# Hybrid attention trunk on one core: psT from three banks to two, psO from one bank to two

## The chip, the cores and the metric

The kernel runs on one core of one Trainium2 chip. The metric is device time in microseconds (us), lower is better; the time before is the median of 3 runs. A profile is one execution of its own, with the time of each instruction on each engine. PE is TensorE, DVE is VectorE, ACT is ScalarE, POOL is GpSimd, SP is SyncE, which here issues nearly all the DMAs.

## The reference

One layer over x of 1024 tokens by 1024 features, fp32. Three groups of 8 heads of size 64 share one input projection and one output projection:

```python
h = rmsnorm(x, norm_g)
proj = h @ w_in                 # q, k, v, gate for each group, forget logits for one
o_sb = stick_breaking_attention(q_sb, k_sb, v_sb)           # strictly causal
o_ch = chunked_relpos_attention(norm(q_ch), norm(k_ch), v_ch, rel_bias)   # a band of 9 chunks of 64
o_fx = forgetting_attention(norm(q_fx), norm(k_fx), v_fx, log_f)          # causal, with decay
mixed = concat(o_g * silu(gate_g) for g in (sb, ch, fx))
out = x + mixed @ w_out
```

In each attention a weight matrix of queries by keys (scores, then a softmax or the stick-breaking product) multiplies the values of its head.

## The kernel before

**High and low halves.** To keep fp32 accuracy, each matrix is held as a rounded high part and a low part (the fp32 value less the high part). ACT copies the high part out, DVE subtracts it from the source and writes the low part. So each tile that PE has turned (transposed) into PSUM is read twice, first by ACT and then by DVE, and is free only when DVE has ended.

**Pairs, rows and units.** The 24 heads are 12 pairs `j` of two heads `s`. A pair has 16 score blocks `n` (8 blocks of 128 queries for each head). Four blocks make a unit `u`, of which there are 48; unit `u` belongs to pair `u // 4`. For each unit the weight blocks, 128x128 with queries on the partitions, are turned by PE so that keys lie on the partitions, and then multiplied with the values. `banks(u)` says how: a unit is 3, 5 or 7 tiles of up to four blocks. The steps of a unit stand in this order:

```python
    seq = [("turn", u, 0)]
    for b in range(1, len(banks(u))):
        seq += [("turn", u, b), ("values", u, b - 1)]
    return seq + [("values", u, len(banks(u)) - 1)]
```

**The work of one tile.** `turn` (L1287) is up to four transposes on PE from `z` into `psT`; ACT copies the high part into `pt` (L939), DVE subtracts and writes the low part (L1128) and counts `s_evac`. `values` (L1305) waits for that count and multiplies both parts into the sum bank `psO`. When all tiles of a unit are added, `gather` reads `psO`: ACT takes one half of the partitions to `otmp` (L949), DVE adds the other half (L1135, which counts `s_os`) and multiplies with the gate (L1141).

**Who else uses psT.** All turned tiles take the banks of `psT` in one running order `m`, tile `m` in bank `m % NT`, and before tile `m` PE waits for the DVE reading of tile `m - NT`. There are 290 tiles: 16 of `x` (`("x", t)`, two for each t, transposes L1185, read by ACT L786 and DVE L991), 48 of `heads` (queries and keys, L1235, read by ACT L879 with a gain and by DVE L1053), 2 of `forget` (L1244, ACT L896, DVE L1070) and 224 of `turn`. The `heads` tiles then go through two DMAs inside `stack` (L635, L636, then L642, L643) before scores can use them (L1265, L1266).

**PSUM.** There are eight banks of 128x512 fp32: two for scores (`psS`), three for `psT`, one for `psO`, two for projections and the output (`psP`). At the end the output projection rotates over `psP`, `psS` and `psO` (L1353).

**The order.** `plan()` writes out one order of steps at build time, and each engine goes through the same list, doing its own part of each step, in order. Nothing overtakes. Attention steps have hand-set places (`AT`, `OWN`, `NEXT`), and between them `filler` puts pieces of the next pair's projection (L1213 for q, k, v, L1217 for the gate), three matmuls at a time. At the start, steps stand so: `x` 0 and `x` 1 (four tiles), then the first projection pieces; later `x` 7, `heads` (0,0,0) and `forget` 0 stand one behind the other. In the pairs 1 to 4 the second half of the first head's queries and keys stands inside a unit:

```
turn(3,0)=34, project, turn(3,1)=35, project, heads(1,0,1)=36, values(3,0), scores(18), turn(3,2)=37
```

and the same with the numbers of units 7, 11 and 15. From pair 5 on it stands behind the first `values` of the unit (`values(31,0), heads(8,0,1)=190, scores, turn(31,2)=191, values(31,1), project, turn(31,3)=192`). The number is the place `m` in the order of psT.

Of the kernel before, what the change touches and what calls it, by code (L numbers as in the profile page):

```python
# [6 lines left out]
F32 = mybir.dt.float32  # L7
# [3 lines left out]
ACT = mybir.ActivationFunctionType  # L11
AX = mybir.AxisListType

P = 128
# [15 lines left out]
HALF = 512  # L30
# [14 lines left out]
TOKW = FW + QKV  # L45
WP = TOKW + P
WR = 3
NT = 3
PTR = 2


# [327 lines left out]
def build(nc, x, norm_g, w_in, b_forget, q_norm_ch, k_norm_ch, q_norm_fox, k_norm_fox, rel_bias, w_out, out):  # L379
# [5 lines left out]
    with ExitStack() as ctx:  # L385
# [34 lines left out]
        vst = sb("vst", [P, 3, TT, P], F32R)  # L420
# [6 lines left out]
        otmp = sb("otmp", [P, HALF])  # L427
# [15 lines left out]

        psS = ctx.enter_context(nc.psum_tensor("psS", [P, 2 * HALF], F32))
        psT = ctx.enter_context(nc.psum_tensor("psT", [P, NT, HALF], F32))
        psO = ctx.enter_context(nc.psum_tensor("psO", [P, HALF], F32))
        psP = ctx.enter_context(nc.psum_tensor("psP", [P, 2, HALF], F32))


# [16 lines left out]
        def end_tile(t, c):  # L466
            return piece[3 * c + t] if t < 3 else resid[t][:, c * HALF:(c + 1) * HALF]

        endbank = [psP[:, i, :] for i in range(2)] + [psS[:, i * HALF:(i + 1) * HALF] for i in range(2)] + [psO[:, :]]

        s_const = sem("s_const")
        s_identr = sem("s_identr")
# [43 lines left out]
        s_oc = sem("s_oc")  # L516
        s_os = sem("s_os")
# [240 lines left out]
        def _(act):  # L758
# [6 lines left out]
            for step in PLAN:  # L765
# [27 lines left out]
                if kind == "weights":  # L793
                    _, j, k = step
# [3 lines left out]
                    if j:  # L798
# [3 lines left out]
                                         scale=gcol[:, k:k + 1]).then_inc(s_whi, 1)  # L802
                if kind == "gatew":
                    _, j, h = step
# [21 lines left out]
                if kind == "raw":  # L826
                    _, j, t = step
                    u = t // 4
# [18 lines left out]
                if kind == "gate":  # L847
                    _, j, u = step
# [12 lines left out]
                if kind == "sq":  # L861
                    _, j, u = step
# [6 lines left out]
                if kind == "heads":  # L869
                    _, j, s, u = step  # L870
# [5 lines left out]
                    else:  # L876
# [3 lines left out]
                                         scale=gain[:, g:g + 1]).then_inc(s_hi, 1)  # L880
                if kind == "vsplit":
                    _, j, s, u = step
# [5 lines left out]
                if kind == "forget":  # L888
                    _, u = step
# [11 lines left out]
                if kind == "scores" and step[1] >= NSOFT:  # L901
# [3 lines left out]
                    i = n - NSOFT  # L905
# [19 lines left out]
                if kind == "rescale":  # L925
# [4 lines left out]
                                         scale=small[:, n % 8, 3:4]).then_inc(s_pn, 1)  # L930
                if kind == "turn":
                    _, u, b = step
# [7 lines left out]
                if kind == "gather":  # L940
                    _, u = step
                    s = u // 2 % 2
                    rows, other = slice(s * HD, (s + 1) * HD), slice((1 - s) * HD, (2 - s) * HD)
                    act.wait_ge(s_pv, VAL0[u + 1])
                    if u == 0:
                        act.wait_ge(s_fc, 4)
                    if u >= 1:
                        act.wait_ge(s_prod, u)
                    nc.scalar.activation(otmp[rows, :], psO[other, :], ACT.Copy, scale=0.5).then_inc(s_oc, 1)  # L949
                if kind == "mix":  # L950
                    _, j, u = step
                    i = 2 * j + u
# [9 lines left out]
        def _(dve):  # L962
            for step in PLAN:
# [29 lines left out]
                if kind == "weights":  # L993
                    _, j, k = step
# [3 lines left out]
                                                   scalar=gcol[:, k:k + 1], in1=wpair[0][:, k, FW:TOKW].bitcast(F32),  # L998
# [5 lines left out]
                if kind == "gatew":  # L1004
                    _, j, h = step
# [17 lines left out]
                if kind == "gate":  # L1023
                    _, j, u = step
# [3 lines left out]
                                                   in1=psP[:, u, :], op0=ALU.add, op1=ALU.mult).then_inc(s_gate, 1)  # L1028
                if kind == "sq":
                    _, j, u = step  # L1030
                    i = 2 * j + u
# [6 lines left out]
                if kind == "norm" and step[1] < NORMED:  # L1038
                    _, j, u = step
                    i = 2 * j + u  # L1040
                    dve.wait_ge(s_rn, i + 1)
                    r = rs[:, 16 * u:16 * u + 16].rearrange("p (t f s a) -> p t f s a", t=4, f=2, a=1)
                    for f in range(2):
                        ins = nc.vector.tensor_tensor(qk_out(f, u), qk_raw(f, u),
                                                      r[:, :, f, :, :].broadcast_to([P, 4, 2, HD]), ALU.mult)
                    ins.then_inc(s_qn, 1)
                if kind == "heads":
                    _, j, s, u = step
# [5 lines left out]
                        out=stack[:, s, 2, cols], in0=psT[:, m % NT, :], scalar=gain[:, g:g + 1],  # L1054
                        in1=stack[:, s, 1, cols].bitcast(F32), op0=ALU.mult, op1=ALU.subtract).then_inc(s_evac, 1)
                if kind == "vsplit":
                    _, j, s, u = step
                    h = 2 * j + s
                    i = VSPLIT[j, s, u]
# [3 lines left out]
                if kind == "forget":  # L1063
                    _, u = step
# [7 lines left out]
                if kind == "decay":  # L1072
                    _, u = step
# [9 lines left out]
                if kind == "scores" and step[1] < NSOFT:  # L1083
# [3 lines left out]
                    s = n // TT % 2  # L1087
# [10 lines left out]
                    if n >= 8:  # L1098
# [3 lines left out]
                                                   scalar=3.0e38, op0=ALU.add, op1=ALU.min,  # L1102
# [8 lines left out]
                if kind == "weigh" and step[1] >= NSOFT:  # L1111
                    n = step[1]
                    i = n - NSOFT
# [8 lines left out]
                if kind == "turn":  # L1122
                    _, u, b = step
# [6 lines left out]
                if kind == "gather":  # L1130
                    _, u = step
                    s = u // 2 % 2
                    rows = slice(s * HD, (s + 1) * HD)
                    dve.wait_ge(s_oc, u + 1)
                    nc.vector.scalar_tensor_tensor(out=otmp[rows, :], in0=psO[rows, :], scalar=0.5, in1=otmp[rows, :],  # L1135
                                                   op0=ALU.mult, op1=ALU.add).then_inc(s_os, 1)
                    j, h = u // 4, u % 2
                    cols = slice(h * HALF, (h + 1) * HALF)
                    dve.wait_ge(s_gate, 2 * j + h + 1)
                    dve.wait_ge(s_os, u + 1)  # L1140
                    nc.vector.tensor_tensor(gate[rows, j % 2, cols], gate[rows, j % 2, cols], otmp[rows, :],  # L1141
                                            ALU.mult).then_inc(s_prod, 1)
                if kind == "mix":
                    _, j, u = step
# [3 lines left out]
                if kind == "part":  # L1148
                    i = step[1]
# [23 lines left out]
        def _(pe):  # L1173
            pe.wait_ge(s_identr, 1)
            for step in PLAN:
                kind = step[0]
                if kind == "x":
                    _, t = step
                    pe.wait_ge(s_xn, t + 1)
                    for u in range(2):  # L1180
# [3 lines left out]
                        for i in range(4):  # L1184
                            ins = nc.tensor.transpose(psT[:, m % NT, i * P:(i + 1) * P],  # L1185
                                                      xt[t][:, (4 * u + i) * P:(4 * u + i + 1) * P], ident)
                        ins.then_inc(s_turn, 1)
                if kind == "project":
                    _, j, gi, k0, k1 = step
                    what, i = GROUPS[gi]  # L1190
# [3 lines left out]
                    if k0 == 0 and before >= 0:  # L1194
                        jb, gb = divmod(before, NG)
                        kb, ib = GROUPS[gb]
# [8 lines left out]
                    for k in range(k0, k1):  # L1205
# [4 lines left out]
                        for q, (a, b) in enumerate(((0, 0), (0, 1), (1, 0))):  # L1210
                            if what == "t":
                                first = 0 if j == 0 else FW
                                ins = nc.tensor.matmul(dst[:, 0:TOKW - first], hT[a][:, k, i * P:(i + 1) * P],  # L1213
                                                       wpair[b][:, k, first:TOKW],
                                                       start=(k == 0 and q == 0), stop=(k == KT - 1 and q == 2))
                            else:
                                ins = nc.tensor.matmul(dst[:, :], wpair[b][:, k, TOKW:WP],  # L1217
                                                       hT[a][:, k, i * HALF:(i + 1) * HALF],
                                                       start=(k == 0 and q == 0), stop=(k == KT - 1 and q == 2))
# [6 lines left out]
                if kind == "heads":  # L1226
                    _, j, s, u = step
# [6 lines left out]
                    for i in range(4):  # L1234
                        ins = nc.tensor.transpose(psT[:, m % NT, i * P:(i + 1) * P],  # L1235
                                                  qks[:, 4 * u + i, s * P:(s + 1) * P], ident)
                    ins.then_inc(s_turn, 1)
                if kind == "forget":
                    _, u = step
# [3 lines left out]
                    for i in range(4):  # L1243
                        ins = nc.tensor.transpose(psT[0:HG, m % NT, i * P:(i + 1) * P], raw[:, 4 * u + i, 0:FW], ident)  # L1244
                    ins.then_inc(s_turn, 1)
                if kind == "scores":
                    n = step[1]
                    j, s, b = n // 16, n // TT % 2, n % TT
# [12 lines left out]
                    for pi, (col, key, w) in enumerate(parts):  # L1261
# [4 lines left out]
                        ins = nc.tensor.matmul(dst, qs, stack[:, s, 2, key:key + w], start=False, stop=not masked)  # L1266
                        if masked:
                            end = off + P * (b + 1)
                            m0 = 1 - (group(n) == 2)
                            ins = nc.tensor.matmul(psS[:, end - P:end], identb[:, :], mask[:, m0:m0 + P],  # L1270
                                                   start=False, stop=True)
                    ins.then_inc(s_scores, 1)
                if kind == "turn":
                    _, u, b = step
# [8 lines left out]
                    for kb, q0, cnt in banks(u)[b]:  # L1283
                        for q in range(q0, q0 + cnt):
                            n = 4 * u + q
                            at = z_at(n)[0] + (kb - window(n)[0]) * P
                            ins = nc.tensor.transpose(psT[:, m % NT, col:col + P], z[:, at:at + P], ident)  # L1287
                            col += P
                    ins.then_inc(s_turn, 1)
                if kind == "values":  # L1290
                    _, u, b = step
                    ci = VAL0[u] + b
                    j, s, h = u // 4, u // 2 % 2, u % 2
                    nb = len(banks(u))
                    if b == 0:
                        for half in range(h + 1):
                            pe.wait_ge(s_vlo, VSPLIT[j, s, half] + 1)
                        if u:
                            pe.wait_ge(s_os, u)
                    pe.wait_ge(s_evac, last_turn(("turn", u, b)))  # L1300
                    col = 0
                    pieces = banks(u)[b]
                    for pi, (kb, q0, cnt) in enumerate(pieces):
                        for v in range(2):
                            ins = nc.tensor.matmul(psO[:, q0 * P:(q0 + cnt) * P], vst[:, (2 * j + s) % 3, kb, :],  # L1305
                                                   pt[:, ci % PTR, v, col:col + cnt * P], start=(b == 0 and v == 0),
                                                   stop=(b == nb - 1 and v == 1 and pi == len(pieces) - 1))
                        col += cnt * P
                    ins.then_inc(s_pv, 1)
                if kind == "first":  # L1310
                    _, i, k0, k1 = step
# [66 lines left out]
```

## Time and profile before

| | |
|---|---|
| time before | 1053.86 us, median of 3 runs (1053.61 to 1054.18) |
| the profiled execution | 1054.61 us, of which the span from first to last instruction is 1052.8 us |
| granted TensorE clock, mean | 0.996 |
| PE busy | 1017.2 us, 97% of the span |
| DVE busy, ACT busy | 679.9 us (65%), 632.9 us (60%) |
| DMA | 105.50 MB, mean 100 GB/s |

How to read it: the span is what the profile divides up; the time of a run has 1.8 us more around it. A busy share is the time in which the engine had an instruction running. Matmuls are pipelined, so the end of one matmul lies past the start of the next, and the distance of starts is the pace.

### The profile page before, as it was taken

What the parts mean: (1) busy time and instruction counts of PE and PEld (TensorE: products, weight loads), DVE (VectorE), ACT (ScalarE), POOL (GpSimd) and SP (SyncE); (2) the same over time, 40 slices, a digit from 0 to 9 for tenths busy, and PEclk for the clock granted to TensorE, in tenths of its full rate; (3) what the DMA queues carried; (4) which work ended last, traced back from release to release, by engine and by line L of the source; (5) the groups of instructions that cost most, each with busy time, mean ns of one, the idle gap of its engine ahead of it and who ended that gap; (6) DMA issues with size and microseconds to landing.
All of it is one profiled execution on the core that took longest, in us unless ns stands there. A gap on an engine that the chain in (4) does not pass through costs nothing.

```text
span 1052.8 us, 16215 instructions
## 1 busy us (share of the span) xinstructions
PE 1017.2 (97%) x5816; PEld 910.3 (86%) x5816; DVE 679.9 (65%) x1272; ACT 632.9 (60%) x1232; POOL 96.5 (9%) x74
## 2 busy tenths in 40 slices
PE   6999999999999999999999999999999998899998
PEld 5988989899899898998998998998988986687887
DVE  4656675755756756667557548879789786777110
ACT  5658775766766757767667667557567564443000
POOL 1210201101111011011011001011011010000000
PEclk9999999999999999999999999999999998999999
DMA  8244151331432513414314204204214127742941
GB/s 249 82 136 119 38 143 47 105 98 44 128 86 47 146 49 81 121 46 114 90 53 125 76 21 113 68 21 126 56 37 125 48 64 212 215 130 71 312 128 40
DMA packets 112944, 105.50 MB, mean 100 GB/s; under 512 B 10048, under 2 KB 83784, under 8 KB 112864
## 3 DMA queue, kind: packets, MB, share of 16 engines
q1 hardware_dynamic: 110432, 104.42, 35.9%
q8 instruction: 46, 0.75, 0.3%
q10 hardware_dynamic: 2432, 0.05, 0.1%
q14 instruction: 34, 0.28, 0.1%
HBM read 62.44 MB, written 19.98 MB: 78 GB/s over the span
## 4 chain that ended last, share of the span: by engine, by line
PE 76%; DVE 11%; DMA 5%; ACT 4%; issue 3%; SPq 1%; ACTq 0%; DVEq 0%
PE psP L1213 38%; PE psO L1305 8%; PE psT L1287 6%; PE psS L1265 4%; PE psS L1266 4%; PE psP L1217 3%; PE psP L1323 3%; PE psP L1353 2%; PE psS L1353 2%; DVE big L997 2%; PE psT L1235 2%; PE psO L1353 2%; DMA stack<-stack 2%; DVE pt L1128 2%; DVE rb L1117 1%
## 5 line engine op out<-in xcount | busy, mean ns | idle before, releaser
L1213 PE MATMUL psP<-big 128*128 128x384 f32 (+1 forms) x2304 | 478.5, 345 | 1.8 <-DVE big L997 1.3
L1213 PEld LDWEIGHTS psP<-big 128*128 128x128 f32 x2304 | 394.8, 189 | 8.5 <-DVE big L997 1.6
L1128 DVE TENSOR_TENSOR pt<-psT,pt 128x512 fp32r<-128x512 f32 (+1 forms) x224 | 143.1, 641 | 142.0 <-ACT pt L939 141.4
L939 ACT ACTIVATE pt<-psT 128x512 fp32r<-128x512 f32 (+1 forms) x224 | 125.1, 559 | 114.4 <-PE psT L1287 113.5
L1217 PE MATMUL psP<-big 128*128 128x512 f32 x576 | 157.5, 406 | 0.0
L1305 PE MATMUL psO<-pt,vst 128*128 128x512 f32 (+3 forms) x576 | 140.3, 343 | 9.7 <-DVE pt L1128 9.2
L1287 PE MATMUL psT<-identr,z 128*128 128x128 f32 x816 | 125.4, 272 | 0.0
L1305 PEld LDWEIGHTS psO<-pt,vst 128*128 128x128 f32 x576 | 99.0, 189 | 22.3 <-issue 10.9
L1217 PEld LDWEIGHTS psP<-big 128*128 128x128 f32 x576 | 102.0, 189 | 17.7
L1287 PEld LDWEIGHTS psT<-identr,z 128*128 128x128 f32 x816 | 101.6, 140 | 15.4
L1101 DVE CUSTOM_DVE_ANT_0 z<-psS,rb 128x640 f32<-128x640 f32 (+7 forms) x128 | 89.3, 698 | 39.2 <-PE psS L1266 20.6
L1265 PE MATMUL psS<-stack 128*128 128x256 f32 (+3 forms) x288 | 97.8, 347 | 3.1 <-DMA stack<-stack 2.7
L929 ACT ACTIVATE z<-z,small 128x640 f32<-128x640 f32 (+7 forms) x128 | 93.3, 729 | 2.7 <-DVE small L1110 2.4
L1266 PE MATMUL psS<-stack 128*128 128x256 f32 (+3 forms) x288 | 94.9, 332 | 0.0
L923 ACT ACTIVATE z<-z,small 128x640 f32<-128x640 f32 (+7 forms) x128 | 93.1, 728 | 0.7
L1117 DVE TENSOR_TENSOR_SCAN rb<-rb 128x128 f32<-128x128 f32 (+3 forms) x64 | 86.2, 1348 | 0.0
L844 ACT ACTIVATE raw<-psP 128x384 f32<-128x384 f32 x88 | 43.1, 490 | 65.3 <-PE psP L1213 65.2
L738 POOL TENSOR_TENSOR rs<-ms,mhalf 128x16 f32<-128x16 f32 x16 | 48.1, 3006 | 362.7 <-DVE ms L1037 362.7
L914 ACT ACTIVATE rb<-psS 128x128 f32<-128x128 f32 (+3 forms) x64 | 41.8, 653 | 57.4 <-PE psS L1270 57.2
L1265 PEld LDWEIGHTS psS<-stack 128*128 128x128 f32 x288 | 54.2, 188 | 7.7 <-DMA stack<-stack 3.4
L1323 PE MATMUL psP<-big 128*128 128x512 f32 x192 | 53.6, 413 | 7.2 <-DMA big<-mixed_scratch 6.0
L997 DVE SCALAR_TENSOR_TENSOR big<-wraw,gcol,big 128x384 fp32r<-128x384 f32 x90 | 55.6, 619 | 5.2 <-ACT big L801 4.9
(113 smaller groups left out, 1093.5 us busy)
## 6 DMA issues: line engine op xcount, KB each, us to landing
stack<-stack SPq DMA_DIRECT2D x192, 128.0 KB, 2.3
wraw<-in_w_in_dram SPq DMA_DIRECT2D x90, 192.0 KB, 2.6
wraw<-in_w_in_dram SPq DMA_DIRECT2D x24, 256.0 KB, 3.6
mixed_scratch<-mst SPq DMA_DIRECT2D x24, 256.0 KB, 2.7
mixed_scratch<-gate SPq DMA_DIRECT2D x24, 256.0 KB, 2.8
wraw<-in_w_out_dram SPq DMA_DIRECT2D x24, 256.0 KB, 3.1
rb<-decay_scratch SPq DMA_DIRECT2D x8, 512.0 KB, 4.1
big<-mixed_scratch SPq DMA_DIRECT2D x8, 512.0 KB, 6.6
```

Of the source, the lines that this page charges most:

```text
L923: nc.scalar.activation(z[:, at:at + w], z[:, at:at + w], ACT.Exp, scale=-1.0, bias=small[:, q, 0:1], accum_out=small[:, q, 2:3]).then_inc( ...
L929: nc.scalar.activation(z[:, at:at + w], z[:, at:at + w], ACT.Copy, scale=small[:, n % 8, 3:4]).then_inc(s_pn, 1)
L939: nc.scalar.activation(pt[:, ci % PTR, 0, 0:w], psT[:, m % NT, 0:w], ACT.Copy).then_inc(s_hi, 1)
L1101: nc.vector.tensor_tensor_reduce(out=z[:, at:at + w], in0=psS[:, off:off + w], in1=add, scale=1.0, scalar=3.0e38, op0=ALU.add, op1=ALU.min ...
L1117: nc.vector.tensor_tensor_scan(out=back, data0=back, data1=back, initial=1.0, op0=ALU.mult, op1=ALU.bypass).then_inc(s_rem, 1)
L1128: nc.vector.tensor_tensor(pt[:, ci % PTR, 1, 0:w], psT[:, m % NT, 0:w], pt[:, ci % PTR, 0, 0:w].bitcast(F32), ALU.subtract).then_inc(s_eva ...
L1213: ins = nc.tensor.matmul(dst[:, 0:TOKW - first], hT[a][:, k, i * P:(i + 1) * P], wpair[b][:, k, first:TOKW], start=(k == 0 and q == 0), st ...
L1217: ins = nc.tensor.matmul(dst[:, :], wpair[b][:, k, TOKW:WP], hT[a][:, k, i * HALF:(i + 1) * HALF], start=(k == 0 and q == 0), stop=(k == K ...
L1265: nc.tensor.matmul(dst, qs, stack[:, s, 1, key:key + w], start=True, stop=False)
L1266: ins = nc.tensor.matmul(dst, qs, stack[:, s, 2, key:key + w], start=False, stop=not masked)
L1287: ins = nc.tensor.transpose(psT[:, m % NT, col:col + P], z[:, at:at + P], ident)
L1305: ins = nc.tensor.matmul(psO[:, q0 * P:(q0 + cnt) * P], vst[:, (2 * j + s) % 3, kb, :], pt[:, ci % PTR, v, col:col + cnt * P], start=(b == ...
```

## The change

The running order of psT goes over two banks (NT from 3 to 2). The bank set free becomes a second sum bank: psO has two banks, and unit `u` adds in bank `u % 2`. So `turn`, `x`, `heads` and `forget` wait for the DVE reading of the tile two before, where it was three before, and the first `values` of a unit waits for the gather of unit `u - 2`, where it was `u - 1`. No operation is added, removed or moved.

```diff
-NT = 3
+NT = 2
...
-        psO = ctx.enter_context(nc.psum_tensor("psO", [P, HALF], F32))
+        psO = ctx.enter_context(nc.psum_tensor("psO", [P, 2, HALF], F32))
...
-        endbank = [psP[:, i, :] for i in range(2)] + [psS[:, i * HALF:(i + 1) * HALF] for i in range(2)] + [psO[:, :]]
+        endbank = [psP[:, i, :] for i in range(2)] + [psS[:, i * HALF:(i + 1) * HALF] for i in range(2)] + [psO[:, 0, :]]
...
-                    nc.scalar.activation(otmp[rows, :], psO[other, :], ACT.Copy, scale=0.5).then_inc(s_oc, 1)
+                    nc.scalar.activation(otmp[rows, :], psO[other, u % 2, :], ACT.Copy, scale=0.5).then_inc(s_oc, 1)
...
-                    nc.vector.scalar_tensor_tensor(out=otmp[rows, :], in0=psO[rows, :], scalar=0.5, in1=otmp[rows, :],
+                    nc.vector.scalar_tensor_tensor(out=otmp[rows, :], in0=psO[rows, u % 2, :], scalar=0.5, in1=otmp[rows, :],
...
-                        if u:
-                            pe.wait_ge(s_os, u)
+                        if u >= 2:
+                            pe.wait_ge(s_os, u - 1)
...
-                            ins = nc.tensor.matmul(psO[:, q0 * P:(q0 + cnt) * P], vst[:, (2 * j + s) % 3, kb, :],
+                            ins = nc.tensor.matmul(psO[:, u % 2, q0 * P:(q0 + cnt) * P], vst[:, (2 * j + s) % 3, kb, :],
```

The waits of PE that change with NT are `pe.wait_ge(s_evac, m - NT + 1)` ahead of the transposes (L1183, L1233, L1242, L1281).

## Rows read from the trace of the kernel before

**Rows 1.** The page, busy time (share of the span) by engine.

```profile
PE 1017.2 (97%) x5816; PEld 910.3 (86%) x5816; DVE 679.9 (65%) x1272; ACT 632.9 (60%) x1232; POOL 96.5 (9%) x74
```

**Rows 2.** Waits of PE: who waited for whom, us in total, times, longest.

```profile
PE psO L1305 <- DVE pt L1128: 9.2, 18, 1.3
PE psS L1265 <- DMA stack<-stack: 2.7, 3, 1.4
PE psP L1213 <- DVE big L997: 1.3, 1, 1.3
```

**Rows 3.** Timeline round the first values of unit 47 (start, length, engine, line).

```profile
957.05 0.69 DVE L1135 SCALAR_TENSOR_TENSOR otmp<-psO,otmp 64x512 f32<-64x512 f32 x1
...
960.76 0.30 PEld L1305 LDWEIGHTS psO<-pt,vst 128*128 128x128 f32 x2 [1.31 <-issue]
```

**Rows 4.** Timeline at the first tiles of x, PE and DVE.

```profile
11.39 1.97 PE L1185 MATMUL psT<-identr,qks 128*128 128x128 f32 x8 [1.93 <-DVE qks L973]
...
14.78 7.24 PE L1213 MATMUL psP<-big 128*128 128x392 f32 x39 [0.44 <-DVE big L991]
...
11.26 1.28 DVE L991 TENSOR_TENSOR big<-psT,big 128x512 fp32r<-128x512 f32 x2
...
14.03 0.69 DVE L991 TENSOR_TENSOR big<-psT,big 128x512 fp32r<-128x512 f32 x1 [0.16 <-ACT big L786]
```

**Rows 5.** Timeline at x 3, PE and DVE.

```profile
23.12 1.29 DVE L991 TENSOR_TENSOR big<-psT,big 128x512 fp32r<-128x512 f32 x2 [1.29 <-ACT big L786]
...
23.80 1.04 PE L1185 MATMUL psT<-identr,gate 128*128 128x128 f32 x8
```

**Rows 6.** Timeline at heads (0,0,0) and forget 0.

```profile
46.11 0.66 PE L1235 MATMUL psT<-identr,qks 128*128 128x128 f32 x4
46.31 1.28 DVE L991 TENSOR_TENSOR big<-psT,big 128x512 fp32r<-128x512 f32 x2
...
47.14 0.60 PE L1244 MATMUL psT<-identr,raw 128*8 128x128 f32 x4 [0.37 <-ACT raw L846]
...
47.49 1.30 PE L1213 MATMUL psP<-big 128*128 128x392 f32 x6
```

**Rows 7.** Timeline at turn (2,1) and at turn (31,3).

```profile
114.86 0.69 DVE L1128 TENSOR_TENSOR pt<-psT,pt 128x512 fp32r<-128x512 f32 x1 [0.92 <-ACT pt L939]
...
115.46 0.60 PE L1287 MATMUL psT<-identr,z 128*128 128x128 f32 x4
...
642.71 0.60 PE L1287 MATMUL psT<-identr,z 128*128 128x128 f32 x4
...
642.10 0.74 DVE L1053 SCALAR_TENSOR_TENSOR stack<-psT,gain,stack 128x512 fp32r<-128x512 f32 x1
```

**Rows 8.** Timeline of unit 3: PE and DVE round heads (1,0,1).

```profile
132.10 0.60 PE L1235 MATMUL psT<-identr,qks 128*128 128x128 f32 x4
133.14 0.70 PE L1305 MATMUL psO<-pt,vst 128*128 128x512 f32 x2 [0.44 <-DVE pt L1128]
...
132.31 0.68 DVE L1128 TENSOR_TENSOR pt<-psT,pt 128x512 fp32r<-128x512 f32 x1
...
134.04 0.74 DVE L1053 SCALAR_TENSOR_TENSOR stack<-psT,gain,stack 128x512 fp32r<-128x512 f32 x1
```

**Rows 9.** The chain that ended last: start, us, what.

```profile
56.35 0.51 ACT raw L846
...
76.55 0.44 PE psT L1235 x4
...
277.74 4.44 DMA stack<-stack
```

**Rows 10.** Timeline at turn (42,1).

```profile
845.26 0.69 DVE L1128 TENSOR_TENSOR pt<-psT,pt 128x512 fp32r<-128x512 f32 x1 [0.95 <-ACT pt L939]
...
846.11 0.60 PE L1287 MATMUL psT<-identr,z 128*128 128x128 f32 x4
```

**Rows 11.** A stretch: its us, busy PE, PEld, DVE, ACT, POOL; clock, DMA, GB/s.

```profile
882.00:888.00 6.00, 6.00 (x24) 4.82 (x23) 0.69 (x1) 0.82 (x2) 0.00 (x0) 0.78 0.67 211
```

## The prediction

> **What bounds the kernel now.** I read the page first. PE is busy for 97% of the span and DVE for 65% [rows 1]. So any moment in which PE newly stands still is likely to be paid in full, and a bank can only help where PE now waits for one. The next view is therefore the list of PE's waits, and each new or removed wait is then looked at in the timeline of its own place. The reader is to see that, behind the start-up (where PE waits for x), the largest total, 9.2 us in 18 waits, is `values` waiting for DVE's low part in `pt` [rows 2]. No row names a wait for `otmp`, which is what a wait for the sum bank would show as. That decides the gain side almost alone. The loss side has no row, because before there was nearly always a free psT bank: it has to be made from the distance between a tile and the reading two tiles before.
>
> **The sum: the profiled execution.** Its time is 1054.61 us, its span 1052.8 us, so 1.8 us lie around the span; it stands 0.75 us above the median of 1053.86 us. What I find in the span I add to the median.
>
> **Part 1: two sum banks.** The first `values` of a unit may start one unit earlier relative to the gather. What the old wait costs is read where it is tightest. In unit 47 the gather's DVE step ends at 957.05 + 0.69 = 957.74 us, and PE loads the first weights for the new sum at 960.76 us, 3.0 us later [rows 3]. Over all units, laid out in the same way, this is the smallest distance. A wait that is over 3.0 us before it is asked for costs nothing. Could it be worth more? Only if the 18 waits of [rows 2] were put down to the wrong engine, and a semaphore reached 3.0 us ago can't be what ended them. Nothing is queued differently on ACT or DVE either: the gather keeps its place in both, and reads as many elements from PSUM. I take 0; the bound above is the rival below.
>
> The Trainium skill, Perfetto Trace Analysis, section Optimizing Tensor Performance, Matmuls, says that independent matmul groups should rotate through different PSUM banks, so that the evacuation of one overlaps the next group's matmuls. By that rule this half of the change should win time. The trace shows the evacuation already over 3.0 us before the next group, because turns and projections of psP stand between, so by the row it wins nothing [rows 3].
>
> **Part 2: two turning banks.** Within a unit the new wait is mostly no new one. `turn(u,b+1)` stands behind `values(u,b-1)`, and that has already waited for the reading of tile `turn(u,b-1)`, which is the tile two before. So I laid out the order of psT tiles and marked those where no earlier instruction of PE has waited for that reading: 91 of the 290 tiles. For each of these I compared PE's start with DVE's end two tiles back. Most have microseconds to spare. PE would be late at these:
>
> - x 1, the first of its two tiles. It starts at 11.39 us; the tile two before is read until 11.26 + 0.69 = 11.95 us (two readings of 0.69 us lie in the 1.28 us) [rows 4]. From an ended DVE to a starting PE the rows show 0.06 us (14.03 + 0.69 = 14.72, then 14.78) to 0.15 us (132.31 + 0.68 = 132.99, then 133.14) [rows 4, 8]; I take 0.1. So it starts at about 12.0: **+0.6 us**. Its second tile is then late by itself no more. The projection at 14.78 waits for ACT and DVE to read just these tiles [rows 4], so it moves with them.
> - x 3. The second tile starts half way through 1.04 us at 24.24 (starts of 4 transposes take 0.44 [rows 9]); the reading two before ends at 23.12 + 1.29 = 24.41 [rows 5]. **+0.25 us**.
> - heads (0,0,0) and forget 0. heads starts at 46.11, the reading of x 7's first tile ends at 46.31 + 0.69 = 47.0, so it starts at 47.1. forget needs x 7's second tile, read until 46.31 + 1.28 = 47.59, so it starts at 47.65 in place of 47.14, and the projection behind it at 48.0 in place of 47.49 [rows 6]. **+0.5 us**. Before, forget waited there for ACT; so only 0.5 of the 1.0 that heads loses is paid.
> - turn (2,1): start 115.46, reading until 114.86 + 0.69 = 115.55 [rows 7]. **+0.2 us**.
> - turn (31,3): start 642.71, reading of heads (8,0,1) until 642.10 + 0.74 = 642.84 [rows 7]. **+0.2 us**.
> - heads (j,0,1) for j = 1 to 4, the largest term. In unit 3 it starts at 132.10; the tile two before is turn (3,0), read until 132.99. Behind it in PE's order stands `values(3,0)`, which waits for that same reading and starts at 133.14 [rows 8]. So PE's stand of 0.44 us before `values` goes, and one of 0.9 us before `heads` comes. The net is the four transposes that used to run under the wait: their pace is 0.44 us [rows 9]. Units 7, 11 and 15 repeat the pattern of unit 3, with `values` bound by the same reading in each. 4 x 0.44 = **+1.76 us**. Here the new wait holds what is queued behind it on PE: values, the next scores, turn (3,2); ACT's L879, which waits for these transposes, starts about 0.9 us later, and DVE's L1053 about 0.4 later than 134.04 [rows 8], since it stood idle before that start.
>
> The sum is 0.6 + 0.25 + 0.5 + 0.2 + 0.2 + 1.76 = 3.5 us. turn (u,2) in units 3, 7 and 11 also sits within 0.1 us of its reading, but PE arrives there 0.44 us later than before, and so it costs nothing more.
>
> **Is it given back later?** A delay of PE vanishes where PE later waits for something that isn't delayed. Candidates are one wait for weights (1.3 us, in the second pair's first projection) and three for stack (2.7 us) [rows 2]. The chain view says both hang on PE: the first comes from ACT's L846 at 56.35, which reads what PE's projection behind forget has made, over DVE and the weights' DMA; and in pair 3 the chain goes from DVE's L1053 (the reading of the very heads tile that is held) over two DMAs, the second at 277.74, 4.44 us long, to PE's scores [rows 9]. These waits therefore shift with PE and keep their length. What hides them is gone, so I count nothing back; if all were given back the low end follows. The late L1053 is about as late as PE itself (0.4 us), so the stack wait should neither grow.
>
> **No operation changes its length**: the same columns, the same engines, eight banks used before and after. The granted clock fell below full mainly once, behind a stand of PE of almost 4 us for the output projection's operands (0.78 in [rows 11]); the new stands are at most 0.9 us.
>
> **Rivals.**
>
> *Forecast: +3.5 us*, 1053.86 + 3.5 = 1057.3 us. Chance 0.67. Its own range is 1056.1 to 1058.6: release times of 0.06 or 0.15 for the nine places give some 0.4 us each way, and half of one absorbed term the rest.
>
> *The delay is partly given back.* If the 1.3 us for weights takes up the first three terms (1.35 us), 2.15 us are left, 1056.0 us; if the stack waits also take up the heads terms of pairs 1 to 3 (3 x 0.44 = 1.3 us, of their 2.7), 0.8 us are left, 1054.7 us. For it: these waits are really there and end with DMAs, whose length can vary. Against it: the chain of [rows 9]. That the change does nothing at all, because every new wait is already covered, lies here too: 0 us, 1053.9 us; 199 of 290 tiles are so covered, and the rest would have to be. Chance together 0.17.
>
> *Near misses become stalls.* 18 more of the 91 tiles have between 0.16 and 0.5 us to spare, the closest being turn (42,1), read until 845.26 + 0.69 = 845.95 against its start at 846.11 [rows 10]. If the late ACT and DVE work behind each stall stays late by some 0.6 us against PE, each pays about 0.2 us: 18 x 0.2 = 3.6 us more, 1060.9 us. Against it: PE is late itself by nearly as much, and DVE at 65% has room to catch up. Chance 0.11.
>
> *The sum bank was the wait (faster).* The mechanism: first `values` of a unit held by the gather. Its place is the first `values` of a unit, as at 133.14 [rows 8], and its price is some of the 9.2 us, if the trace misnames what ended them. It decides once more than the 3.5 us of part 2 goes, and then at the most 9.2 - 3.5 = 5.7 us are won, 1048.2 us; half of it gives 1052.8. Against it: 3.0 us of distance at the tightest place [rows 3]. Chance 0.05. This is the skill's rule on rotating banks taken at its word.
>
> **How the numbers follow.** The likeliest case gives 1057.3 us. For 8 in 10, I go down into the given-back case to 1055.2 and up past the forecast's range to 1059.6, which leaves out the lower part of the given-back case, the faster one, and most of the near-miss case. 0.2% is 2.1 us, about what a measurement of this kernel can tell from no change; slower begins at 1055.97. Slower: the forecast, the near misses, 0.67 + 0.11 = 0.78. Same: 0.17. Faster: 0.05.
>
> **What would show it.** In the waits of PE: L1235 with a new wait for DVE L1128 of about 0.9 us in four places, L1185 with one for L991 of some 0.6 us, and the waits of L1305 for L1128 down by about 1.5 us, since those of units 3, 7, 11 and 15 go. Projection pieces after 47 us should start 1.35 us later than before, those after unit 15 about 3.3 us later, those at the end 3.5 us. The gather's distance to the next unit's values plays no part. The prediction is wrong if the wait for weights shrinks by as much as PE is late, if L1287 shows more than one or two waits for DVE, or if the waits of L1305 fall outside those four units.

## The result

| | median | executions |
|---|---|---|
| before | 1053.86 us | 7 (1051.22 to 1055.80) |
| changed | 1058.55 us | 7 (1056.71 to 1062.25) |

The ratio is 1.0046, with a 95% interval from 1.0027 to 1.0066: slower by 4.8 us (2.8 to 7.0), where 3.5 us were forecast (1057.3 us, range 1055.2 to 1059.6). Taken once more on another occasion the same kernel gave 1.0047 (1.0035 to 1.0059).

The profiled execution has a span of 1055.1 us, 2.3 us more than before. The page of the changed kernel, busy time by engine:

```profile
PE 1018.1 (96%) x5816; PEld 910.7 (86%) x5816; DVE 680.0 (64%) x1272; ACT 632.8 (60%) x1232; POOL 95.7 (9%) x74
```

No busy time grew beyond 1 us, against [rows 1]; what grew is PE's idle time. Who PE waited for in the changed kernel (us in total, times, longest; waits of lesser bearing left out):

```profile
PE psO L1305 <- DVE pt L1128: 7.3, 12, 1.3
...
PE psT L1235 <- DVE pt L1128: 3.3, 4, 0.9
PE psT L1185 <- DVE big L991: 2.6, 1, 2.6
PE psP L1213 <- DVE big L997: 2.2, 1, 2.2
...
PE psT L1235 <- DVE big L991: 1.1, 1, 1.1
```

Rows 2, 3 and 5 of these are waits for a psT bank, which before had none. The 2.6 us of the third are not all new: PE stood 1.93 us at the same place before, for DVE's L973 [rows 4]. The first row has six waits and 1.9 us less than before. Four of the six are those of units 3, 7, 11 and 15, where now heads stands in place of `values` (the second row). A fifth is at 648 us, told below; the sixth shrank from 0.17 to 0.15 us, which the view no longer counts. The wait for weights (L1213 for L997) grew from 1.3 to 2.2 us.

Round unit 3 the timeline of PE and of DVE in the changed kernel reads:

```profile
136.25 0.63 PE L1235 MATMUL psT<-identr,qks 128*128 128x128 f32 x4 [0.87 <-DVE pt L1128]
136.63 0.71 PE L1305 MATMUL psO<-pt,vst 128*128 128x512 f32 x2
```
```profile
135.42 0.68 DVE L1128 TENSOR_TENSOR pt<-psT,pt 128x512 fp32r<-128x512 f32 x1
137.70 0.75 DVE L1053 SCALAR_TENSOR_TENSOR stack<-psT,gain,stack 128x512 fp32r<-128x512 f32 x1 [0.47 <-ACT stack L879]
```

Against [rows 8], the same reading (ended at 136.10) now releases the transposes, and `values` follows them after 0.38 us with no wait of its own.

**A ledger of PE's lag.** PE has the same instructions in the same order in both kernels, so the n-th can be laid against the n-th. The lag is its start in one kernel less its start in the first profile of before; its growth over a place is what the place cost. In us, for the changed kernel (two profiles), for two experiments told below (late_start has only the new waits up to 47 us, late_heads only those of heads in pairs 1 to 4), and for a second profile of before:

| place | changed | changed, again | late_start | late_heads | before, again |
|---|---|---|---|---|---|
| x 1 | +0.65 | +0.66 | +0.65 | -0.02 | -0.02 |
| x 3 | +0.28 | +0.28 | +0.28 | -0.01 | 0.00 |
| heads (0,0,0), forget 0 | +0.61 | +0.60 | +0.60 | +0.03 | 0.00 |
| wait for weights | +0.89 | +0.96 | +0.32 | +0.88 | -0.25 |
| turn (2,1) | +0.21 | +0.21 | 0.00 | 0.00 | 0.00 |
| unit 3 | +0.39 | +0.38 | 0.00 | +0.40 | +0.01 |
| unit 7 | +0.38 | +0.38 | -0.01 | +0.39 | 0.00 |
| unit 11 | +0.40 | +0.39 | 0.00 | +0.40 | 0.00 |
| unit 15 | +0.38 | +0.38 | -0.01 | +0.39 | -0.01 |
| turn (31,3) | +0.25 | +0.25 | 0.00 | 0.00 | 0.00 |
| values, 5 us behind turn (31,3) | -0.26 | -0.27 | 0.00 | -0.01 | 0.00 |

The psT places repeat to 0.02 us wherever their wait is in the kernel, and are 0 where it is not. In the changed kernel they add up to 0.65 + 0.28 + 0.61 + 0.21 + 0.39 + 0.38 + 0.40 + 0.38 + 0.25 = 3.55 us.

Of these 3.55 us, the 0.25 us of turn (31,3) are given back at once. The `values` that follow 5 us later waited for DVE in the kernel before, and wait no more in the changed one (PE, before and changed):

```profile
647.98 0.73 PE L1305 MATMUL psO<-pt,vst 128*128 128x512 f32 x2 [0.17 <-DVE pt L1128]
```
```profile
651.89 0.72 PE L1305 MATMUL psO<-pt,vst 128*128 128x512 f32 x2
```

The transposes of that tile start at 646.50 and 650.66 us, so the distance to `values` is 1.48 us before and 1.23 us after. It shrinks in the three profiles in which turn (31,3) is late (by 0.26, 0.27 and 0.26 us), and by at most 0.04 us in all others. So 3.3 us of the 3.55 stay.

The places that end with a DMA do not repeat: the waits for stack together took 2.7 us in the first profile of before, 2.0 and 0.7 in two more, and 2.1 and 1.8 in two of the changed kernel; the wait for the output projection's operands 3.9, 3.1 and 2.1 us before, 2.5 and 3.5 changed. This scatter is large enough for one pair of profiles to show 2.3 us where the medians of 7 executions differ by 4.7.

### The profile page after: what moved, and what is told of

The parts are those of the page before. It is cut to its first block, busy times and chain, and to the rows that moved or that the text cites. A ratio compares the mean times of both kernels' runs of the same rounds, so it can differ in the third digit from the quotient of the medians.

```text
span 1055.1 us, 16215 instructions
## 1 busy us (share of the span) xinstructions
PE 1018.1 (96%) x5816; PEld 910.7 (86%) x5816; DVE 680.0 (64%) x1272; ACT 632.8 (60%) x1232; POOL 95.7 (9%) x74
## 4 chain that ended last, share of the span: by engine, by line
PE 76%; DVE 10%; DMA 4%; ACT 4%; issue 3%; SPq 1%; POOL 0%; ACTq 0%; DVEq 0%; POOLq 0%
PE psP L1213 37%; PE psO L1305 8%; PE psT L1287 7%; PE psS L1265 4%; PE psP L1217 4%; PE psS L1266 4%; PE psP L1323 3%; PE psP L1353 2%; PE psS L1353 2%; PE psT L1235 2%; DVE big L997 2%; PE psO L1353 2%; DMA stack<-stack 1%; DVE pt L1128 1%; DVE rb L1117 1%
## 5 line engine op out<-in xcount | busy, mean ns | idle before, releaser
L1213 PE MATMUL psP<-big 128*128 128x384 f32 (+1 forms) x2304 | 479.3, 346 | 2.7 <-DVE big L997 2.2
L1213 PEld LDWEIGHTS psP<-big 128*128 128x128 f32 x2304 | 395.7, 189 | 9.3 <-DVE big L997 2.5
L1128 DVE TENSOR_TENSOR pt<-psT,pt 128x512 fp32r<-128x512 f32 (+1 forms) x224 | 143.2, 641 | 141.2 <-ACT pt L939 140.6
L1305 PE MATMUL psO<-pt,vst 128*128 128x512 f32 (+3 forms) x576 | 140.3, 343 | 8.0 <-DVE pt L1128 7.3
L1305 PEld LDWEIGHTS psO<-pt,vst 128*128 128x128 f32 x576 | 99.1, 189 | 19.6 <-issue 8.5
L997 DVE SCALAR_TENSOR_TENSOR big<-wraw,gcol,big 128x384 fp32r<-128x384 f32 x90 | 55.6, 620 | 6.3 <-ACT big L801 6.0
```

The lines of the kernel that those rows point to most:

```text
L1128: nc.vector.tensor_tensor(pt[:, ci % PTR, 1, 0:w], psT[:, m % NT, 0:w], pt[:, ci % PTR, 0, 0:w].bitcast(F32), ALU.subtract).then_inc(s_eva ...
L1305: ins = nc.tensor.matmul(psO[:, u % 2, q0 * P:(q0 + cnt) * P], vst[:, (2 * j + s) % 3, kb, :], pt[:, ci % PTR, v, col:col + cnt * P], star ...
```

## The experiments

**The first half of the change alone.** Two turning banks, one sum bank, the gather's wait as before.

```diff
-NT = 3
+NT = 2
```

> Only the first half of the change: two banks for turned tiles, one sum bank, and the wait of values for the gather as before (one PSUM bank lies unused). Theory (the second sum bank is worth nothing, since the gather is over 3.0 us before it is asked for): the same as the changed kernel, +3.5 us against before by the stalls, +4.8 us by the measured ratio, and in the profile the same four waits of L1235 for DVE L1128 (0.87, 0.88, 0.88 and 0.65 us in the changed kernel), with values L1305 waiting for DVE L1128 alone. Rival (the second sum bank wins a part and hides a larger loss): slower than the changed kernel by over 1 us, with waits of L1305 for DVE otmp L1135.

Measured: ratio 1.0050 (1.0034 to 1.0066), as the changed kernel. Its waits, by the same view:

```profile
PE psO L1305 <- DVE pt L1128: 7.5, 13, 1.4
...
PE psT L1235 <- DVE pt L1128: 3.3, 4, 0.9
```

No wait for otmp appears with one sum bank, and the nine psT places cost 3.55 us here too. The second sum bank is worth nothing that shows (1.0050 without it, 1.0046 and 1.0047 with it, inside each other's intervals); the loss comes with the two banks of psT.

**The waits of heads alone**, with three banks kept.

```diff
-                    pe.wait_ge(s_evac, m - NT + 1)
+                    pe.wait_ge(s_evac, m - (2 if 1 <= j <= 4 and (s, u) == (0, 1) else NT) + 1)
```

> The kernel before with all its banks, but in pairs 1 to 4 PE waits ahead of heads (j,0,1) for the reading of the tile two before, where it was three. Theory (the four transposes that ran under the wait of values are laid bare, 0.44 us each): +1.8 us in all; PE's start of values in units 3, 7, 11 and 15 moves by 0.38 to 0.45 us in each, and the waits of L1305 there turn into waits of L1235 of 0.65 to 0.88 us. Rival (the delay of the heads tiles goes through their DMAs into the waits of scores for stack, and is paid at their full 0.9 us, or the waits of scores give it back): +3.3 us, or 0.

Measured: ratio 1.0028 (1.0016 to 1.0039), +2.9 us; the four places cost 1.58 us, and no stack wait grew with them. So the theory holds for the places, and the whole is above what it gave. Eight of the eleven executions lie at 1054.2 to 1056.6 us, mean 1055.4, 2.0 us above the mean of the 21 executions of before beside them (1053.4); three lie at 1058.8 to 1059.8 with a lower mean clock (0.994). The profile is of one of the three: before its first changed wait, its transfer of weights is long (5.15 us) and PE's clock falls at the wait for it. That this is also the story of the other two is not shown.

**The waits of the start alone**, up to 47 us.

```diff
-                        if m >= NT:
-                            pe.wait_ge(s_evac, m - NT + 1)
+                        if m >= 2:
+                            pe.wait_ge(s_evac, m - 2 + 1)
...
-                    pe.wait_ge(s_evac, m - NT + 1)
+                    pe.wait_ge(s_evac, m - (2 if j == 0 else NT) + 1)
...
-                    pe.wait_ge(s_evac, m - NT + 1)
+                    pe.wait_ge(s_evac, m - 2 + 1)
```

> The kernel before with all its banks, but up to 47 us PE waits for the reading of the tile two before (x, heads of pair 0 and forget). Theory of the prediction: the three stalls 0.6, 0.25 and 0.5 us, +1.35 us. Theory that the profile of the changed kernel suggests: the same stalls (0.68, 0.36 and 0.54 us, 1.6 us), and on top of them PE runs its first projection matmuls at half clock for longer, because the later start leaves fewer of them done when the clock rises: 0.6 us more in an execution where that happens, +2.2 us. Rival (the wait for weights behind it takes it up): PE's start at that wait is late, its end is not, 0 to +0.5 us.

Measured: ratio 1.0029 (1.0014 to 1.0044), +3.1 us. The three places cost 1.53 us; the wait for weights took none of it back and was 1.65 us long. The matmuls at half clock at the start of the first projection did come (1.2 us more of lag), but see the next run.

**Both kernels once more**, each for a second profile, with nothing edited.

> The changed kernel once more, for a second profile. The stalls of PE at the places with psT waits must repeat to within 0.05 us if they are the program's own. The waits that end with a DMA (weights at 76 us, stack at 146 and 216 us, the output projection's operands at 884 us) differed from before by -1.3 to +0.9 us; theory: these are the scatter of DMA lengths and come out otherwise here, by up to 1 us each. Rival: they are caused by the change, and come out as in the first profile (2.2, 0.9, 1.1, none at 286, 2.5 us).

> The kernel before once more, for a second profile. In the first one PE waited 1.3 us for weights at 72.90 us, and the four other kernels profiled since waited 1.7 to 2.3 us there, the one with an unchanged start (late_heads) 2.2 us. Theory (scatter of the DMA, the first profile was a lucky one there): about 2.2 us now, with the stalls at psT absent as before, and the clock's rise at the start may come some matmuls later than at 15 us, as in late_heads, for up to 1 us. Rival (the change made this wait longer): 1.3 us again, and no matmul at half clock behind 15 us.

Measured: changed 1.0047 (1.0035 to 1.0059), before 1.0002 (0.9988 to 1.0016). The psT places repeated. The start at half clock did not: the second profile of the changed kernel has none of it, the kernels with an unchanged start have 0 to 1.2 us. That is scatter of when the clock rises, and falls out. The wait for weights was 1.08 us before, not 2.2, and 2.29 us changed. So my theory that the first profile had been a lucky one was wrong, and the rival that the wait is longer with the change stood.

**The transfer of weights.** Two more kernels: late_x has only the first hunk of the start's diff, late_heads_zero only the other two, and both the start's kernel (late_start) and before were profiled again.

> The kernel before with all its banks; only the tiles of x wait for the reading of the tile two before. Both theories expect the stalls themselves, 0.68 us at x 1 and 0.2 to 0.35 us at x 3. What is open is the transfer of the last weights but two of pair 1 (issued about 20 us behind the first half of pair 0's heads): with an unchanged start it took 4.26, 4.02, 4.09, 4.10 and once 5.15 us, with the tight start 5.13, 5.22, 5.26, 4.88 and 4.56 us, and PE's wait for it follows. Theory (scatter): between 4.0 and 5.3 us, whatever waits. Rival (the tight waits lengthen it, by the later heads): 4.0 to 4.3 us here, since the heads wait as before. Whole: +1.0 us, +0.9 more if it is long.

> The kernel before with all its banks; only heads of pair 0 and the two forget tiles wait for the reading of the tile two before. The stall: heads starts 0.9 to 1.1 us later, the projection behind it 0.53 to 0.65 us. Theory (scatter): the weights' transfer takes 4.0 to 5.3 us. Rival (the later heads lengthen it): 4.6 to 5.3 us. Whole: +0.6 us, or +1.4.

> The kernel before, for a third profile: one more draw of the weights' transfer with an unchanged start. Rival (tight waits lengthen it): 4.0 to 4.3 us. Theory (scatter): anything from 4.0 to 5.3 us.

> The kernel with the tight start once more, for a second profile: one more draw of the weights' transfer. Rival (tight waits lengthen it): 4.6 to 5.3 us. Theory (scatter): anything from 4.0 to 5.3 us.

Measured: late_x 1.0016 (1.0002 to 1.0029), late_heads_zero 1.0003 (0.9992 to 1.0014). Their places cost 0.65 + 0.28 and 0.60 us. The two further profiles are of single executions, 1050.99 us before and 1056.83 us late_start. Each profile is one draw: that of late_x is of its longest execution (1058.72 us), that of late_heads_zero of its shortest (1051.59 us). The chain that ended last holds the transfer in all of them; its piece in the third profile of before and in late_x:

```profile
67.30 4.24 DMA wraw<-in_w_in_dram
```
```profile
68.91 5.59 DMA wraw<-in_w_in_dram
```

The transfer's length from issue to landing in all 14 profiles, in us (heads moved: the kernels of the last experiment below):

| x waits as before | x waits for two tiles back |
|---|---|
| before 4.26, 4.02, 4.24 | changed 5.13, 5.22 |
| heads moved, three banks 4.09, 4.11 | one sum bank 5.26 |
| late_heads_zero 4.04 | late_start 4.56, 5.32 |
| late_heads 5.15 | late_x 5.59; heads moved, two banks 4.89 |
| mean 4.27 | mean 5.14 |

The rival as I had put it (by the later heads of pair 0) fell, as far as one profile can say: late_heads_zero holds these heads and has a short transfer, and in whole time it can't be told from before. The long ones go with the waits of x, in seven of seven, against one of seven without. Nothing in SP's order differs.

What the traces do show beside a long transfer is one more packet. The profile lists a DMA queue q8 of kind instruction, which moves one packet of 16 KB every 20 us or so. While the transfer runs in before (67.24 to 71.50 us) only q1, the program's own queue, moves anything; in late_heads (68.04 to 73.19 us) the list of queues has this row too (packets, MB, share of 16 engines):

```profile
q8 instruction: 1, 0.02, 1.2%
```

In all eight profiles with 4.56 us or more, late_heads among them, such a packet starts inside the transfer, at 70.7 to 72.3 us, and takes 0.9 to 1.2 us. In all six with 4.02 to 4.26 us it starts at 74.8 to 75.8 us, behind the landing. The means are 5.14 against 4.13 us, 1.0 us apart, which is about what that packet takes. In late_start, with 4.56 us the shortest of the eight, the packet comes early in the transfer, with more than half of the transfer's 384 packets of 512 B still to start after it has ended; in the other seven it is 23 to about 40 of them. So the packet goes with the length in 14 of 14, better than the waits of x do in 13 of 14. That the one delays the other is argued from this, for no run moves the packet alone. Nor is it shown what brings the packet forward: it is early in all seven profiles with the late x, and in late_heads without it.

**What the longer wait does to the clock.** Stretches of the trace (us; busy PE, PEld, DVE, ACT, POOL with instructions; granted clock; DMA share; GB/s) behind the wait, in before, in the second profile of the changed kernel and in late_x:

```profile
76.00:79.00 3.00, 3.00 (x22) 2.96 (x21) 0.75 (x1) 2.41 (x4) 0.88 (x2) 1.00 0.90 278
```
```profile
76.00:79.00 3.00, 3.00 (x14) 3.00 (x13) 0.84 (x3) 0.00 (x0) 1.04 (x1) 0.62 0.80 216
```
```profile
76.00:79.00 3.00, 3.00 (x10) 3.00 (x11) 0.16 (x1) 0.41 (x2) 1.04 (x1) 0.50 0.93 241
```

PE is as busy in all three. With a granted clock of 0.50, which is 1.2 GHz in place of 2.4, it gets through 10 matmuls in place of 22; with 0.62 over the stretch, through 14. Over the matmuls from 72.9 to 76.5 us in before the lag grew by 1.4 us in the second of these and by 2.6 us in the third, beside the longer wait. PE had stood 2.2 us or more before it in six of the 14 profiles (2.21, 2.22, 2.29, 2.32, 2.38, 2.67 us), and the clock fell in four of them, during the stand or within 1.4 us of its end; in the eight with stands of 1.1 to 2.0 us it fell in none.

**The heads moved.** In pairs 5 to 10 the third bank was used for what it is good for: heads (j,0,1) put ahead of the first `values` of its unit, so that four transposes run under that wait. The same lines were added to the changed kernel, and with range(1, 5) to before, where they put heads behind the first `values` in pairs 1 to 4:

```diff
 PLAN = plan()
+for _j in range(5, 11):
+    PLAN.insert(PLAN.index(("values", 4 * _j - 1, 0)), PLAN.pop(PLAN.index(("heads", _j, 0, 1))))
```

> The kernel before (three turning banks) with heads (j,0,1) put ahead of the first values of its unit in pairs 5 to 10, as it already stands in pairs 1 to 4; no work left out. Theory (a free third bank lets four transposes of 0.44 us run under the wait of values, 0.66 us in pairs 5 to 7, 0.17 to 0.22 us in pairs 8 to 10): 3 x 0.44 + 0.17 + 2 x 0.2 = -1.9 us. Rival (the wait of values ends with DVE, which now gets the same work later or in another order, or PE's wait only moves on to the next tile): 0.

> The changed kernel (two turning banks) with the same move in pairs 5 to 10. Theory (with two banks heads waits for the very reading that values waits for, so the move hides nothing): 0 against the changed kernel, with the waits of L1305 in units 19, 23 and 27 (0.66 us) turned into waits of L1235 of the same length. Rival (the move itself helps, whatever the banks): -1.9 us against the changed kernel.

> The kernel before (three turning banks) with heads (j,0,1) put behind the first values of its unit in pairs 1 to 4. Nothing waits for a psT bank then. Theory (what the change costs there is only that four transposes no longer run under the wait of values): +0.38 to +0.45 us in each of the four, 1.55 us in all, as in late_heads, with waits of L1305 of 0.88, 0.88, 0.88 and 0.66 us. Rival (the change's cost there is of the bank's wait itself, by what it holds up on ACT and DVE): under 0.5 us in all.

Unit 19 in before, with three banks and the move, and with two banks and the move (timeline of PE):

```profile
415.82 0.71 PE L1305 MATMUL psO<-pt,vst 128*128 128x512 f32 x2 [0.67 <-DVE pt L1128]
416.36 0.60 PE L1235 MATMUL psT<-identr,qks 128*128 128x128 f32 x4
```
```profile
414.75 0.60 PE L1235 MATMUL psT<-identr,qks 128*128 128x128 f32 x4
415.56 0.71 PE L1305 MATMUL psO<-pt,vst 128*128 128x512 f32 x2 [0.22 <-DVE pt L1128]
```
```profile
420.59 0.63 PE L1235 MATMUL psT<-identr,qks 128*128 128x128 f32 x4 [0.67 <-DVE pt L1128]
420.97 0.71 PE L1305 MATMUL psO<-pt,vst 128*128 128x512 f32 x2
```

With three banks the transposes fill 0.44 us of the 0.67; with two they wait for the very same reading, and the 0.67 us only changes its owner. By the ledger the six places gave -0.44, -0.43, -0.44, -0.05, -0.44 and -0.42 us, 2.2 us in all, near the 1.9 expected but not place by place. In pair 8 `values` had no wait to fill; in pairs 9 and 10 the listed wait of 0.22 us was too small a bound, because it counts from the modelled end of the matmul before, 0.6 us behind its start. With two banks, against the changed kernel, the six places gave -0.04, -0.06, -0.07, -0.30, -0.02 and -0.03 us. The -0.30 holds the 0.25 us of turn (31,3), which is no longer late; and just as this goes, the wait of `values` at 648 us is back with 0.17 us, so that nothing is won. In whole times: 0.9990 (0.9972 to 1.0008) with three, which is under before but not clear of it, and 1.0043 (1.0025 to 1.0060) with two, as the changed kernel. The opposite move, where no psT wait exists, cost 0.45, 0.44, 0.44 and 0.44 us in the four units: slightly more than the 0.38 to 0.40 us that the change costs there, in waits of `values` alone. It measured 1.0036 (1.0020 to 1.0052), +3.8 us, above the 1.6 us expected. Its profile has a new wait for stack in pair 4, of 1.5 us, which before had not; that it accounts for the rest in the other executions is likely, not shown:

```profile
355.98 0.38 PE L1265 MATMUL psS<-stack 128*128 128x256 f32 x1 [1.54 <-DMA stack<-stack]
```

## Why the prediction was right, and what in it was not

The forecast of 3.5 us was right in its main part: the new waits for psT stand where it put them, at the cost that it gave, and 3.3 us of the measured 4.8 are theirs. The rest is a wait that it held to be of constant length, and perhaps the clock behind it.

**Gain side, 0.** Right, and shown by the kernel with one sum bank. At the tightest place the changed kernel's gather and the next values stand as in [rows 3] (timelines of DVE and PE):

```profile
959.18 0.70 DVE L1135 SCALAR_TENSOR_TENSOR otmp<-psO,otmp 64x512 f32<-64x512 f32 x1
```
```profile
962.92 0.70 PE L1305 MATMUL psO<-pt,vst 128*128 128x512 f32 x2 [0.92 <-DVE pt L1128]
```

3.0 us of distance again, and the wait is still for the low part. The Trainium skill's rule on rotating PSUM banks (Perfetto Trace Analysis, Optimizing Tensor Performance, Matmuls) is there so that the evacuation of one group overlaps the matmuls of the next. In this kernel the evacuation ends 3.0 us or more before the next group in both versions, and the runs show no gain from it.

**Loss side, term by term** (forecast, measured by the ledger): x 1 0.6, 0.65; x 3 0.25, 0.28; heads (0,0,0) and forget 0.5, 0.61; turn (2,1) 0.2, 0.21; turn (31,3) 0.2, 0.25; heads in four units 1.76, 1.55. The sum is 3.5 against 3.55 us. Each group of four transposes cost 0.39 and not 0.44 us, because behind a stand their pace is quicker (0.38 us from 136.25 to 136.63). That it is these transposes, laid bare, and nothing of the bank itself is shown by the opposite move, which has no bank wait and costs 0.44 us a unit, the transposes' full pace. The release times were 0.15 us at the places of x 1 and heads and 0.06 us at the turns and x 3; 0.1 was taken.

**Given back.** The prediction looked for waits that could absorb a delay among those for weights and stack alone. It left out the waits of `values` for DVE, and one of these, at 648 us, took back all 0.25 us of turn (31,3); by the prediction's own sign (a wait of L1305 that falls outside the four units) this was an error, of 0.26 us. The waits for stack shift with PE and scatter by more than the question; late_heads shows no change of theirs (-0.02, -0.09 and -0.15 us). The wait for weights is where the prediction failed: it was said to shift with PE and keep its length, and it grew by about 0.9 us, the mean transfer of 5.14 against 4.27 us. It goes with the stall of x, and in every profile with a 16 KB instruction packet inside the transfer; what moves that packet is open.

**The clock.** The prediction let new stands of 0.9 us cost nothing at the clock, and no fall stands behind one of them. But the longer wait for weights goes with a fall in four of six profiles. Over all timed executions the mean granted clock is 0.9962 before (84) and 0.9954 changed (12); 0.0008 of 1055 us is 0.8 us of lost matmul time. Together 3.3 + 0.9 + 0.8 = 5.0 us, beside 4.8 us as the difference of the means (1058.6 and 1053.8). The last term is argued, not shown: the single executions range from 0.992 to 0.998, both kernels have further falls at 877 to 891 us and some at 899 to 905 us whose lengths vary, and with 12 executions the difference of the clocks is not clear of scatter.

**Near misses.** None became a stall. turn (42,1) still has 0.16 us and the next five, with 0.26 to 0.30 us, kept theirs within 0.02, since PE is late by what ACT and DVE are late. **Given-back case and faster case**: neither came as a whole; of the first, the 0.26 us above did. The waits of L1305 for L1128 fell from 9.2 to 7.3 us, where 1.5 less were forecast.

## What to carry to other kernels

Before giving a buffer to a tensor, look how long before its next use the old one was free; here the distance was 3 us, and a second buffer bought nothing. For the loss, list in program order which waits are already covered by an earlier wait of the same engine, and lay the rest against the reading they need: nine places of 290 tiles carried all of it, and each came out within about 0.1 us (the four heads together within about 0.2). Then look behind each place for any wait, short ones too, that can take the delay back: one of the nine was returned 5 us later by a wait of 0.17 us. A wait that only changes its owner still costs the work that used to run under it. A spare bank lets work be put ahead of such a wait: moving heads there gave 2.2 us by the ledger, though the whole time (0.9990, 0.9972 to 1.0008) is not clear of no change. And a transfer that PE waits for may change its length without any change in the DMAs that the program issues: list every queue over its stretch.

## What the runs showed of the hardware

One transfer of 192 KB took 4.0 to 4.3 us in the six profiles where no packet of the instruction queue q8 started inside it, and 4.6 to 5.6 us in the eight where one did (16 KB, 0.9 to 1.2 us). The eight are all seven profiles with a stall of 0.65 us some 55 us earlier, and one of the seven without. PE's granted clock fell to 0.5 (1.2 GHz) at stands of 2.2 to 2.7 us in four of six cases, for 1.4 to 2.6 us of lost time each. The point in the first projection at which the clock rose moved by up to 1.2 us of matmul time between executions, with no relation to the edits.
